# Norm sums split between VectorE and TensorE, and one power chain for two adjacent norms

## The reference

```
def rmsnorm(x, w):
    y = x * rsqrt(mean(x * x, axis=-1) + EPS)
    return y * w

# layer 1
h  = rmsnorm(x, norm1_w);  ... attention, gated linear attention, MoBA ...; x = x + mix @ w_out
h2 = rmsnorm(x, norm2_w);  x = x + square(relu(h2 @ w_ff1)) @ w_ff2
x  = rmsnorm(x, final_norm_w)
# layer 2, mod = silu(c) @ w_ada + b_ada, split into shift1, scale1, gate1, shift2, scale2, gate2
h  = rmsnorm(x, norm1_g) * (1 + scale1) + shift1;  proj = h @ w_in;  ... RG-LRU, latent attention ...
x  = x + gate1 * (merged @ w_out)
h2 = rmsnorm(x, norm2_g) * (1 + scale2) + shift2;  x = x + gate2 * (conv gated unit) @ w_down
return rmsnorm(x, final_g)
```

## Time and profile before

| | us |
|---|---|
| median of 3 runs | 1637.77 |
| lowest and highest | 1636.78, 1639.42 |
| profiled execution | 1640.32 |
| its span, first to last instruction | 1638.5 |

### The profile page before, as it was taken

How to read it: one execution, slowest core, us unless ns; L and a number is a source line. 1 busy time by engine, 2 the same in 40 slices (tenths; PEclk the granted TensorE clock), 3 DMA queues, 4 the chain that set the end, 5 groups by cost and what they waited for, 6 DMA issues and landing times.

```text
span 1638.5 us, 21510 instructions
## 1 busy us (share of the span) xinstructions
PE 1536.2 (94%) x6910; PEld 1190.6 (73%) x6910; DVE 928.7 (57%) x1300; ACT 575.7 (35%) x917; POOL 725.3 (44%) x366
## 2 busy tenths in 40 slices
PE   6988967999999999999988999999899999999997
PEld 4765634777888878778766777666687888888885
DVE  5299967368263544786568351666446655564121
ACT  3321255243131323332476332655223323232222
POOL 1589834434444444434323434544243444444442
PEclk7999979999999999999999999999999999999998
DMA  5589820135455555533323324311132333333332
GB/s 190 145 188 198 209 65 27 55 113 167 158 157 166 151 164 153 166 92 86 83 60 93 83 65 104 53 34 39 47 95 64 103 90 102 90 102 89 91 93 86
DMA packets 285060, 176.72 MB, mean 108 GB/s; under 512 B 43794, under 2 KB 269458, under 8 KB 282954
## 3 DMA queue, kind: packets, MB, share of 16 engines
q1 hardware_dynamic: 285002, 175.98, 38.7%
HBM read 173.29 MB, written 5.80 MB: 109 GB/s over the span
## 4 chain that ended last, share of the span: by engine, by line
PE 45%; issue 33%; POOL 11%; DVE 5%; ACT 3%; DMA 2%; SPq 0%; POOLq 0%; DVEq 0%; ACTq 0%
PE ps L1791 13%; PE ps L1793 12%; PE ps L1792 12%; POOL WL L634 9%; DMA vb<-bv_dram 2%; PE ps L2158 2%; PE ps L2001 1%; DVE scanned L1333 1%; PE ps L2169 1%; PE ps L1975 1%; POOL kvp L662 1%; PE ps L2182 1%; DVE qs L1341 1%; ACT LP L883 1%; DVE LP L1395 1%
## 5 line engine op out<-in xcount | busy, mean ns | idle before, releaser
L634 POOL TENSOR_TENSOR WL<-Wraw,WH 128x1024 fp32r<-128x1024 f32 (+2 forms) x239 | 573.1, 2398 | 815.5 <-ACT WH L755 812.0
L1791 PE MATMUL ps<-actH,WH 128*128 128x512 f32 x1256 | 503.9, 401 | 33.3 <-POOL WL L634 14.9
L755 ACT ACTIVATE WH<-Wraw 128x1024 fp32r<-128x1024 f32 (+2 forms) x239 | 246.1, 1031 | 748.8 <-PE ps L1793 658.9
L1792 PE MATMUL ps<-actL,WH 128*128 128x512 f32 x1256 | 493.0, 393 | 0.0
L1793 PE MATMUL ps<-actH,WL 128*128 128x512 f32 x1256 | 492.8, 392 | 0.0
L1791 PEld LDWEIGHTS ps<-actH,WH 128*128 128x128 f32 x1256 | 238.0, 189 | 115.2 <-issue 25.1
L1793 PEld LDWEIGHTS ps<-actH,WL 128*128 128x128 f32 x1256 | 238.0, 189 | 51.2
L1792 PEld LDWEIGHTS ps<-actL,WH 128*128 128x128 f32 x1256 | 238.4, 190 | 48.6 <-issue 1.9
L1791 PE MATMUL ps<-UH,WH 128*128 128x512 f32 x576 | 231.6, 402 | 9.5 <-DVE T L1647 3.9
L1793 PE MATMUL ps<-UH,WL 128*128 128x512 f32 x576 | 228.6, 397 | 0.0
L1792 PE MATMUL ps<-UL,WH 128*128 128x512 f32 x576 | 228.5, 397 | 0.0
(11 more groups left out here) (232 smaller groups left out, 1541.3 us busy)
## 6 DMA issues: line engine op xcount, KB each, us to landing
Wraw<-in_w_ff SPq DMA_DIRECT2D x64, 512.0 KB, 4.1
Wraw<-in_w_in SPq DMA_DIRECT2D x56, 512.0 KB, 4.0
wada<-in_w_ada SPq DMA_DIRECT2D x64, 384.0 KB, 4.2
Wraw<-in_w_up SPq DMA_DIRECT2D x44, 512.0 KB, 3.8
vb<-bv_dram SPq DMA_DIRECT2D x64, 256.0 KB, 4.6
Wraw<-in_w_down SPq DMA_DIRECT2D x16, 448.0 KB, 3.8
Wraw<-in_w_proj_rnn SPq DMA_DIRECT2D x16, 320.0 KB, 3.1
Wraw<-in_w_proj_mla SPq DMA_DIRECT2D x8, 512.0 KB, 4.1
```

The lines of the kernel that those rows point to most:

```text
L634: nc.gpsimd.tensor_tensor(WL[slot][:, 0:kts, :], Wraw[slot][:, 0:kts, :], WH[slot][:, 0:kts, :].bitcast(F32), ALU.subtract).then_inc(s_lo, 1)
L755: A(WH[slot][:, 0:kts, :], Wraw[slot][:, 0:kts, :], ACT.Copy).then_inc(s_hi, 1)
L1791: MM(o, wh, ah, start=first, stop=False)
L1792: MM(o, wh, al, start=False, stop=False)
```

## The change

For `n2` to `n6` VectorE sums only the first seven squares, TensorE turns that sum into columns (`sum_first`, bank 2 or 4), and it turns the eighth square into columns of its own (`sum_last`, bank 5, 6 or 3). VectorE makes the mean of the first half while it waits, and adds the second. ScalarE's last square stands ahead of the weight copy that it stood behind. `norm_factors` has 4 warm-ups instead of 13, between the two column sums. The last rounds of the loops around it are written out.

Between the layers the factor of `n4` comes in one step, from (sum4 / D + EPS * mean3) to the power -0.5, so both powers stand side by side, `n4` first. They stand between the two weight subtractions of the first blocks of `gX` on GpSimd. Each of the last two modulation chunks stands ahead of the add into x. The first seven modulation sums are added before the norm's means, and the eighth, with its own bank 7, is made on TensorE behind the spread of `n4` and added on VectorE behind the normalization.

```diff
+ADA_LATE = 7
-        rtok = keep("rtok", [P, 4, TB])
+        rtok = keep("rtok", [P, 6, TB])
...
-            lows(gX, 2, 1)
+            lows(gX, 1, 1)
+            power("n4", 2)
             power("n3")
-            power("n4", 2)
+            lows(gX, 1, 1, first=1)
...
                     for j in range(2):
-                        if last:
-                            next_high(j)
-                        else:
+                        if last and j == 0:
+                            next_high(0)
+                        elif not last:
                             high(ph, 2 + j, 2 * i + (ph.n0 + 2 + j), landed(ph, 2 + j, i))
                         square(name, 2 * i + j, j, (s_ev, 2 * i + (ph.b0 + j + 1)))
+                    if last:
+                        next_high(1)
...
-            for j in range(2):
-                high(gX, j, gX.n0 + j, landed(gX, j))
-                final_squares(KT // 2 - 1, j)
+            high(gX, 0, gX.n0, landed(gX, 0))
+            final_squares(KT // 2 - 1, 0)
+            final_squares(KT // 2 - 1, 1)
+            high(gX, 1, gX.n0 + 1, landed(gX, 1))
...
-                if isinstance(k, int) and k == 0:
+                if isinstance(k, int) and (k == 0 or k == KT - 1 and name != "n1"):
                     return
...
+                dve.wait_ge(*N(name, "started", 1))
+                own.done(V.tensor_scalar(rtok[:, 4, :], ps[:, first, 0:TB], 1.0 / D_MODEL, EPS, ALU.mult, ALU.add))
                 dve.wait_ge(*N(name, "summed", 1))
-                V.tensor_scalar(rtok[:, at, :], ps[:, bank, 0:TB], 1.0 / D_MODEL, EPS, ALU.mult, ALU.add
-                                ).then_inc(S("norm_mean"), 1)
+                V.scalar_tensor_tensor(rtok[:, 0, :], ps[:, last, 0:TB], 1.0 / D_MODEL, rtok[:, 4, :], ALU.mult, ALU.add
+                                       ).then_inc(S("norm_mean"), 1)
...
                         for j in range(2):
+                            if final:
+                                ada_chunk(o, gi, 1, p, j, h)
...
                             V.tensor_tensor(x, ps[:, two.bank(j), :], x, ALU.add).then_inc(S("x_added"), 1)
-                            ada_chunk(o, gi, 1, p, j, h)
+                            if not final:
+                                ada_chunk(o, gi, 1, p, j, h)
...
-            mean("n3")
-            dve.wait_ge(*N("n3", "power", 1))
-            own.done(V.tensor_tensor(rtok[:, 2, :], rtok[:, 1, :], rtok[:, 1, :], ALU.mult))
-            dve.wait_ge(*N("n4", "summed", 1))
-            own.done(V.tensor_tensor(rtok[:, 2, :], ps[:, 4, 0:TB], rtok[:, 2, :], ALU.mult))
-            V.tensor_scalar(rtok[:, 2, :], rtok[:, 2, :], 1.0 / D_MODEL, EPS, ALU.mult, ALU.add).then_inc(S("norm_mean"), 1)
-
-            dve.wait_ge(S("ada_summed"), 2 * FF_GROUPS)
-            own.done(V.tensor_tensor(mod[:], ps[:, 3, 0:6 * KT], vec[:, VEC["b_ada_2"]:VEC["b_ada_2"] + 6 * KT], ALU.add))
+            dve.wait_ge(S("ada_summed"), ADA_LATE)
+            own.done(modulation(0, early, 3))
...
-            dve.wait_ge(*N("n4", "power", 1))
-            V.tensor_tensor(rtok[:, 3, :], rtok[:, 3, :], rtok[:, 1, :], ALU.mult).then_inc(S("n4_scale"), 1)
-            dve.wait_ge(*N("n3", "spread", 1))
+            dve.wait_ge(*N("n3", "started", 1))
+            own.done(V.tensor_scalar(rtok[:, 4, :], ps[:, 2, 0:TB], 1.0 / D_MODEL, EPS, ALU.mult, ALU.add))
+            own.done(V.tensor_scalar(rtok[:, 5, :], rtok[:, 4, :], EPS, None, ALU.mult))
+            dve.wait_ge(*N("n4", "started", 1))
+            own.done(V.scalar_tensor_tensor(rtok[:, 5, :], ps[:, 4, 0:TB], 1.0 / D_MODEL, rtok[:, 5, :], ALU.mult, ALU.add))
+            dve.wait_ge(*N("n3", "summed", 1))
+            own.done(V.scalar_tensor_tensor(rtok[:, 5, :], ps[:, 5, 0:TB], EPS / D_MODEL, rtok[:, 5, :], ALU.mult, ALU.add))
+            dve.wait_ge(*N("n4", "summed", 1))
+            V.scalar_tensor_tensor(rtok[:, 2, :], ps[:, 6, 0:TB], 1.0 / D_MODEL, rtok[:, 5, :], ALU.mult, ALU.add
+                                   ).then_inc(S("norm_mean"), 1)
+            V.scalar_tensor_tensor(rtok[:, 0, :], ps[:, 5, 0:TB], 1.0 / D_MODEL, rtok[:, 4, :], ALU.mult, ALU.add
+                                   ).then_inc(S("norm_mean"), 1)
+            dve.wait_ge(*N("n4", "spread", 1))
             norm_split("n4", KT, lambda k: xT[:, k, :], lambda k: gainA[:, 0, k:k + 1], lambda k: actL[:, k, :],
                        lambda k: actH[:, k, :], shift=lambda k: mod[:, k:k + 1], bank=4)
-            dve.wait_ge(*N("n4", "spread", 1))
+            dve.wait_ge(*N("n3", "spread", 1))
             own.done(V.tensor_copy(rstd[:], ps[:, 2, :]))
+            dve.wait_ge(S("ada_summed"), 2 * FF_GROUPS)
+            own.done(modulation(early, 6 * KT, 7))
...
+            def norm_columns(k, bank):
+
                 for t in range(TB):
+                    mm = MM(ps[:, bank, t:t + 1], T[k][:, t * P:(t + 1) * P], ones[:, 0:1], start=True, stop=True)
+                return mm
+
+            def sum_first(name, acc=5, bank=2):
+
+                pe.wait_ge(*N(name, "added", KT - 2))
+                norm_columns(acc, bank).then_inc(S("norm_started"), 1)
+
+            def sum_last(name, last=1, bank=5):
+
+                pe.wait_ge(*N(name, "squared", KT))
+                norm_columns(last, bank).then_inc(S("norm_summed"), 1)
...
-                keep_clock(13)
-                norm_sum(name)
+                sum_first(name)
+                keep_clock(4)
+                sum_last(name)
                 keep_clock(5)
...
-            keep_clock(13)
-            norm_sum("n3")
-            norm_sum("n4", 4, 4)
-            ada_sums(2 * FF_GROUPS - 1)
-            spread("n4", (S("n4_scale"), 1), 4, 3)
+            sum_first("n3")
+            sum_first("n4", 4, 4)
+            sum_last("n3")
+            sum_last("n4", 3, 6)
+            keep_clock(4)
+            spread("n4", N("n4", "power", 1), 4, 3)
+            for f in range(ADA_LATE, 2 * FF_GROUPS):
+                ada_sums(f)
             spread("n3", N("n3", "power", 1))
-            keep_clock(7)
...
             turn_rows(KT - 1, 1)
-            norm_sum("n6")
+            sum_first("n6")
+            sum_last("n6", bank=3)
```

49 lines of the change are left out of this document (31 added, 18 removed).

## The result

| | before | change |
|---|---|---|
| median, 6 runs each (us) | 1638.95 | 1622.32 |
| lowest and highest | 1636.78, 1639.42 | 1619.46, 1626.48 |
| profiled execution, span | 1640.32, 1638.5 | 1622.39, 1620.6 |

A forecast was written before the change was run, and what follows sets the result against it. The start of VectorE's normalization between the layers was taken as the bound. Terms -1.06 - 1.01 - 4.2 + 0.7 = -5.6 us gave 1634.7 for the profiled execution, 1632.2 for the median; range 1628.9 to 1635.8.

The forecast's parts named there:

- Norm 2: At 338 us, the last column set starts at 340.0 instead of 341.06, 1.06 us earlier.
- Norm 5: At 1249 us, the last column set starts at 1249.70 instead of 1250.71, 1.01 us earlier.
- Norms 3 and 4: Between the layers at 718 us, VectorE's normalization starts earlier; 4.2 us won, bounds 2.3 and 4.9.
- Norm 6: At the end, both column sets stand behind the last row-tile turn; costs 0.7 us, 1.6 if the clock falls earlier.
- The rest: Written-out last rounds, 64 bytes more for `rtok` and new banks: no engine at its limit sees them, nothing priced.
- the sign of it: Among the signs of a wrong forecast: the stretches between the norms changed in length; no size given.
- rival (a): Between the layers at 718 us the clock stays full: -6.2 us, time 1631.5; chance 0.26.
- the warm-ups hold the spread for 0.4 us: Between the layers, four warm-ups take 1.9 us at half clock, end at 723.7 and delay the spread 0.4.
- Rival (b): Little gained: products behind norm 3 start late, 2.3 instead of 4.2; norms 2 and 5 win half; 1635.5; chance 0.17.
- Rival (c): Slower: the clock falls at norms 2 and 5 too, 1642.9 us, or 1640.1 without the products' part; chance 0.07.
- Rival (d): No effect at 718 us, since something else released the columns; given no chance of its own beside (b).
- The hold: Between the layers, GpSimd's weight subtraction wholly holds VectorE's two-SBUF-input add; if shared by halves, the term is nearer 3.5.

The follow-up runs named there:

- experiment 14: The change with experiment 5's edit and 192 unused bytes ahead of the region that holds `UH` and `UL`; 1631.54 us, ratio to before 0.9948.
- experiment 1: The kernel before with only `rtok` six wide instead of four, so every buffer behind it starts 64 bytes later; 1628.11 against 1638.50 us, ratio 0.9941.
- experiment 9: The change without any warm-up matmuls at norms 2 and 5; 1623.22 us, ratio to before 0.9919.
- experiment 8: The kernel before with GpSimd's second weight subtraction between the layers moved behind both powers; 1637.02 us against 1638.22, ratio 0.9996.
- experiment 6: The kernel before with 64 unused bytes ahead of `WH`, so the weights and `U` move and `act` stays; 1658.79 against 1638.22 us, ratio 1.0129.
- experiment 7: The kernel before with 64 unused bytes ahead of `actH` and `rtok` six wide, so `act`, weights and `U` all start at 192; 1629.23 us, ratio 0.9941.
- experiment 15: The change with experiment 5's edit and 256 unused bytes ahead of the region that holds `UH` and `UL`; 1621.46 us.
- experiment 5: The change with norm 6's first column set ahead of the last row-tile turn instead of behind it; 1621.95 us, ratio to before 0.9894.

## Why the prediction was wrong

**The priced terms held in sum, two of them with luck.** Norm 2: 1.11 instead of 1.06. Norm 5: 1.11 instead of 1.01. Norms 3 and 4: 3.96 instead of 4.2, where executions with the same instructions give 3.1 to 5.0. Norm 6: +0.67 instead of +0.7, but this is luck: the forecast priced the second set at full clock and got 0.7, and at full clock it costs about 0.2; the other 0.5 is a fall of the clock. Sum -5.5 against -5.6, and the trace of experiment 14, with the order of the change at before's distance, gives 5.8. What bounds the kernel before between the layers, the start of VectorE's normalization, was read rightly, down to the spread at 5.1 us behind the last product in the change.

**The step that failed** stands under *The rest*: "the 64 bytes more for `rtok` [...]: no engine at its limit sees them". The engine at its limit is TensorE, and it sees them. The bytes put `UH` and `UL` at distance 0 from the weights, and this took 5 to 6 ns off each of their products: 10.4 us in experiment 1 (7 to 12 by its interval), which has this and nothing else, and 9.3 in its trace (4.0 in the feed-forward, 2.1 between norms 3 and 5, 3.2 behind norm 5). 5.6 and 10.4 make 16.0 of the 16.6 measured. The forecast had named the sign of it, stretches between the norms changed in length, and this sign came. The trace of before did hold a hint that was not followed: 397 ns for `UL` and 393 for `actL`, two groups of one shape and one code line. The range was bounded by the unknown costs of norms; an edit costed at nothing had no bound of its own. The same line put the written-out last rounds at nothing, and at norm 6 the turn starts 0.35 us earlier where they stand. Two sums in the prediction do not come out as they are worded: the lower bound of 1628.9 is rival (a) less the 2.6 us that the runs span, where 1.3 gives 1630.2; and 4.5 - 0.4 makes 3.9 with 0.2 taken off, not with a little added. Neither touches the outcome.

**The norms' details.** That the warm-ups hold the spread for 0.4 us did not come, as the row shows a wait for the power; in its place TensorE's queue cost 0.5 where 0.2 was given. That GpSimd holds the first low part at full clock could not show in the change, since the clock fell. **The clock** went as the forecast took it and not as rival (a): it was at half from about 716 on, although TensorE had no idle stretch of over 0.2 us ahead of it, only sets of one-column matmuls and eight warm-up passes. The Trainium skill (TensorE: Matmul & The Clock Gate, Part 1) says that activity releases the throttle; by that rule, with a column taken for activity, the clock would have stayed full, and the trace differs. Rival (b), late products, came true only in its first half: the queue was the bound, for 0.5 us. Rival (c) did not occur, clock 1.00 at both norms, and in experiment 9 such a fall costs 0.8 for each, counted from the change. Rival (d) falls: the start of VectorE moved by the full 4.48.

**The hold.** The prediction took the hold for whole from its rows, and gave another price for one shared by halves. Experiment 8 says whole: 1.30 us for two sums of 512 columns with GpSimd idle, and 2.22 for one operation on four with GpSimd busy. The Trainium skill (Trainium Architecture — The Big Picture, What this means for kernel authors) calls it an exclusive lock and no split of the bandwidth; the runs agree.

**What stays open.** Why the distance matters is not shown. The Trainium skill (TensorE: Matmul & The Clock Gate, Step-by-step: what each phase is for) says that TensorE reads the streamed operand and the weights through two independent ports, so that loading the next weights takes nothing from the running product. By that rule no distance should matter; experiments 6 and 7, which differ in where the weights stand against the streamed operands, differ by 5 ns in the means of both kinds of product. That the two reads meet in the memory is a guess that fits and that no run tested. Why `UH` and `UL` differ at +64 is open too. So are the small attention products: `PT_odd` on `Vtok` has a mean of 643 ns in before, 618 in the change and in experiment 14, and 676 in experiments 6 and 15, which the distances above do not order. They are part of the 3.8 us between norms 3 and 5 (432 products on `U` at 5.5 ns make 2.4 of it), and probably of the 2.0 us by which that stretch is longer in experiment 15 than in experiment 5.

## What to carry to other kernels

Count the size of a buffer as an edit of every buffer placed behind it: run the layout alone, once with and once without, before the gain of a reordering is believed or given up. Where one engine is busy for 94% of the span, compare its groups of one shape with each other; two means that differ by 1% in one code line are a lead worth more than a whole norm. And move a held operation only after asking which operation is due next beside the holder.
